# Rotary embedding in an eight-sublayer float32 kernel: half-turned copies by transfers within SBUF in place of matrix products

## What is computed

```python
def rope(x, positions):
    half = x.shape[-1] // 2                       # 32
    inv_freq = ROPE_THETA ** (-jnp.arange(half, dtype=jnp.float32) / half)
    ang = positions.astype(jnp.float32)[:, :, None] * inv_freq
    cos = jnp.cos(ang)[:, :, None, :]
    sin = jnp.sin(ang)[:, :, None, :]
    xf = x.astype(jnp.float32)
    x1, x2 = xf[..., :half], xf[..., half:]
    return jnp.concatenate([x1 * cos - x2 * sin, x2 * cos + x1 * sin], axis=-1).astype(x.dtype)
```

## Time and profile before

| | us |
|---|---|
| median of 3 runs | 3043.06 (3040.68 to 3043.27) |
| the profiled execution | 3038.69 |
| its span, first to last instruction | 3036.9 |
| TensorE busy | 3004.3 (99%) |
| VectorE busy | 1773.7 (58%) |
| ScalarE busy | 1267.4 (42%) |
| GpSimd busy | 146.0 (5%) |
| mean granted TensorE clock, share of full | 0.991 |
| q1, the queue of the weights | 254.52 MB, 26.6% of 16 DMA engines |

### The profile page before, as it was taken

One profiled execution on the slowest core, in us unless ns is written; L12 is line 12 of the kernel. 1 busy time (PEld: TensorE's weight loads), 2 busy tenths in 40 slices (PEclk: granted clock), 3 DMA queues, 4 the chain that ended last, 5 costly groups with the idle time before them and its releaser, 6 DMA issues.

```text
span 3036.9 us, 37846 instructions
## 1 busy us (share of the span) xinstructions
PE 3004.3 (99%) x14656; PEld 2400.7 (79%) x14656; DVE 1773.7 (58%) x3123; ACT 1267.4 (42%) x2374; POOL 146.0 (5%) x203
## 2 busy tenths in 40 slices
PE   9999999999999999999999999999999999999998
PEld 7678888878888888888876677888788766788886
DVE  4565775345555577634465557775364655577743
ACT  4444443322333344332366534543233655354431
POOL 1000000000000000001001101000020011010000
PEclk9999999999999999999999999999999999999999
DMA  4122323322222333333211132322232111223332
GB/s 158 61 98 95 100 98 97 97 77 83 84 77 85 96 98 97 98 97 96 94 36 42 48 98 77 104 97 97 84 99 91 34 44 49 90 84 104 97 97 70
DMA packets 72035, 260.35 MB, mean 86 GB/s; under 512 B 8112, under 2 KB 8112, under 8 KB 71728
## 3 DMA queue, kind: packets, MB, share of 16 engines
q1 hardware_dynamic: 70992, 254.52, 26.6%
q10 hardware_dynamic: 864, 3.41, 0.3%
HBM read 255.81 MB, written 2.10 MB: 85 GB/s over the span
## 4 chain that ended last, share of the span: by engine, by line
PE 93%; DVE 4%; ACT 2%; issue 1%; DMA 0%; POOL 0%; SPq 0%; DVEq 0%
PE bank L469 25%; PE bank L472 24%; PE bank L476 24%; PE bank L546 2%; PE bank L550 2%; PE bank L547 2%; PE bank L626 2%; PE bank L658 2%; PE bank L640 1%; PE bank L782 1%; PE bank L899 1%; DVE wl L1356 1%; DVE big L1931 1%; PE bank L929 1%; PE bank L581 1%
## 5 line engine op out<-in xcount | busy, mean ns | idle before, releaser
L1356 DVE TENSOR_TENSOR wl<-ring,wh 128x512 fp32r<-128x512 f32 (+1 forms) x944 | 647.6, 692 | 822.1 <-ACT wh L985 817.3
L469 PE MATMUL bank<-xh,wh 128*128 128x512 f32 x2464 | 987.7, 401 | 14.2 <-ACT xh L992 7.2
L472 PE MATMUL bank<-xh,wl 128*128 128x512 f32 x2464 | 965.3, 392 | 0.3 <-DVE wl L1356 0.3
L476 PE MATMUL bank<-xl,wh 128*128 128x512 f32 x2464 | 925.7, 391 | 0.0
L985 ACT ACTIVATE wh<-ring 128x512 fp32r<-128x512 f32 (+1 forms) x944 | 579.6, 622 | 807.7 <-PE bank L476 726.4
L469 PEld LDWEIGHTS bank<-xh,wh 128*128 128x128 f32 x2464 | 465.4, 189 | 149.6 <-issue 38.4
L476 PEld LDWEIGHTS bank<-xl,wh 128*128 128x128 f32 x2464 | 465.0, 189 | 100.3 <-DVE xl L1449 0.4
L472 PEld LDWEIGHTS bank<-xh,wl 128*128 128x128 f32 x2464 | 466.0, 189 | 91.1 <-DVE wl L1356 1.3
L469 PE MATMUL bank<-bigr,wh 128*128 128x512 f32 x1024 | 399.0, 390 | 0.6 <-ACT bigr L1339 0.6
L472 PE MATMUL bank<-bigr,wl 128*128 128x512 f32 x1024 | 398.4, 389 | 0.0
L476 PE MATMUL bank<-bigr,wh 128*128 128x512 f32 x1024 | 393.4, 389 | 0.0
(11 more groups left out here) (199 smaller groups left out, 2767.9 us busy)
## 6 DMA issues: line engine op xcount, KB each, us to landing
ring<-in_w_up SPq DMA_DIRECT2D x176, 512.0 KB, 3.5
ring<-in_w_down SPq DMA_DIRECT2D x88, 512.0 KB, 3.5
ring<-in_w_in SPq DMA_DIRECT2D x64, 512.0 KB, 3.5
ring<-in_w_ret SPq DMA_DIRECT2D x32, 512.0 KB, 3.3
ring<-in_w_even SPq DMA_DIRECT2D x19, 512.0 KB, 3.4
ring<-in_w_ret_v SPq DMA_DIRECT2D x16, 512.0 KB, 3.3
ring<-in_w_ret_out SPq DMA_DIRECT2D x16, 512.0 KB, 3.4
ring<-in_w_proj SPq DMA_DIRECT2D x16, 512.0 KB, 3.5
```

The costliest lines, as they stand in the source:

```text
L469: e.matmul(o, K.wh(p, c * 128, 128), oh, start=start, stop=False, skip_group_check=True)
L472: e.matmul(o, K.wl(p, c * 128, 128), oh, start=False, stop=False, skip_group_check=True)
L476: m = e.matmul(o, K.wh(p, c * 128, 128), ol, start=False, stop=stop, skip_group_check=True)
L1356: e.tensor_tensor(K.wl(i, 0, w), K.raw(i), K.wh(i, 0, w).bitcast(F32), ALU.subtract).then_inc(F.lo.tell(("piece", i)), 1)
```

## The change

Each half-turned tile is now written by four transfers of 32 partitions within SBUF, issued by SP, from the scratch tile into a tile of its own in `PP` (`turned(r)`). The minus sign moves from the permutation into `invf`, and so into the sines. TensorE's products and their banks go away. SP gets a wait on VectorE's scaling r ahead of each four transfers; the transfers for r = 0 and 1 stand ahead of unit u+1 in SP's program, those for 2 and 3 ahead of u+2, for 4 ahead of u+3, for 5 and 6 ahead of u+4. Two flags, rot0 for even and rot1 for odd r, tell that the transfers have landed. VectorE's multiplication by the sines reads and writes `turned(r)` in SBUF.

```diff
-for _name, _n in (("ident", 128), ("ones", 128), ("tri", 128), ("neg", 128), ("rot", 128), ("blk", 2), ("mhalf", 64),
+for _name, _n in (("ident", 128), ("ones", 128), ("tri", 128), ("neg", 128), ("blk", 2), ("mhalf", 64),
...
+    def turned(self, r):
+
+        return self.PP[:, r * S:(r + 1) * S]
+
+    def turning(self, r):
+        return (self.F.rot0, self.F.rot1)[r % 2]
...
+    def half_turn(l, r):
+
+        q.wait_ge(F.dve, ("ra", l, r))
+        for a, b in ((0, 32), (32, 0), (64, 96), (96, 64)):
+            e.dma_start(K.turned(r)[a:a + 32, :], K.tmp(2 * r % 4)[b:b + 32, :]).then_inc(
+                K.turning(r).tell(*([("rot", l, r)] if a == 96 else []), by=16), 16)
+
+    turns = {}
+    for l in range(2):
+        u = W.raws["w1", l, 0]
+        turns.update({u + 1: (l, (0, 1)), u + 2: (l, (2, 3)), u + 3: (l, (4,)), u + 4: (l, (5, 6))})
     for u, (src, width, pieces) in enumerate(W.units):
+        if u in turns:
+            for r in turns[u][1]:
+                half_turn(turns[u][0], r)
...
-        def rotated(r):
-
-            b = 2 + (r + 1) % 2
-            q.wait_ge(F.dve, ("ra", l, r))
-            empty(b)
-            e.matmul(BK[b][:, :], K.cs("rot"), K.tmp(2 * r % 4), start=True, stop=True).then_inc(F.attn.tell(("rot", l, r)), 1)
-            vacated[b] = [(F.dve, ("rb", l, r))]
-
...
-        rotated(0)
-        rotated(1)
         tile(("n", l, 6), DT, xn(s), F.dve)
-        rotated(2)
-        rotated(3)
         tile(("n", l, 7), DT, xn(s), F.dve)
-        rotated(4)
...
-            if i == 0:
-                rotated(5)
-                rotated(6)
...
         def rope(r):
-            q.wait_ge(F.attn, ("rot", l, r))
-            e.tensor_tensor(K.tmp(2 * r % 4 + 1), BK[2 + (r + 1) % 2][:, :], K.ROPE[:, S:2 * S], ALU.mult).then_inc(
-                F.dve.tell(("rb", l, r)), 1)
+            q.wait_ge(K.turning(r), ("rot", l, r))
+            e.tensor_tensor(K.turned(r), K.turned(r), K.ROPE[:, S:2 * S], ALU.mult).then_inc(F.dve.tell(("rb", l, r)), 1)
             q.wait_ge(F.dve, ("rb", l, r))
             q.wait_ge(F.pool, ("ra", l, r))
-            e.tensor_tensor(K.ropes[r], K.tmp(2 * r % 4), K.tmp(2 * r % 4 + 1), ALU.add).then_inc(
+            e.tensor_tensor(K.ropes[r], K.tmp(2 * r % 4), K.turned(r), ALU.add).then_inc(
                 F.dve.tell(("rope", l, r)), 1)
...
         def rope(r):
             q.wait_ge(F.dve, ("ra", l, r))
-            q.wait_ge(F.attn, ("rot", l, r))
+            q.wait_ge(K.turning(r), ("rot", l, r))
             e.tensor_tensor(K.tmp(2 * r % 4), K.tmp(2 * r % 4), K.ROPE[:, 0:S], ALU.mult).then_inc(
...
-    put("invf", np.tile(inv, 4)[:, None])
+    put("invf", np.tile(np.concatenate([-inv, inv]), 2)[:, None])
```

More of the change, by code:

```diff
@@ L45 @@
 FLAGS = ("proj", "stat", "attn", "hi", "act", "lo", "dve", "pool", "land0", "land1", "land2", "land3",
-         "x0", "first", "x1", "x2", "x3", "x4", "gain", "cst", "vec", "pos", "dil", "ret", "out")
+         "rot0", "rot1", "x0", "first", "x1", "x2", "x3", "x4", "gain", "cst", "vec", "pos", "dil", "ret", "out")
 class Flag:
@@ L2048, in constants @@
     put("neg", -np.ones((128, 128)))
[L2049 to L2055, removed]
     put("blk", (p[:, None] // 64 == np.arange(2)[None, :]).astype(np.float32))
```

## The result

The changed kernel is slower: 3050.18 us median of 9 runs (3048.98 to 3055.19) against 3039.39 for the kernel before in 9 runs (3035.44 to 3043.27). The ratio is 1.0035, 95% interval 1.0025 to 1.0044, or +10.8 us. Forecast were 3041 us and a range of 3032 to 3048, so both the side and the range were missed. The forecast was counted from a median of 3043.06 in three runs; the kernel before is 3.7 us lower in these nine, so the change itself is the better measure: -2.2 us forecast, +10.8 measured. The profiled executions are 3049.32 and 3038.69 us, 10.6 apart, so the traces hold the whole loss.

A forecast was written before the change was run, and what follows sets the result against it. TensorE, busy 99% of the span, was taken to bound the kernel. After 12.4 us of products removed and the new waits, layer 0 nets -3.0 and layer 1 +0.8: -2.2 from 3043.06 gives 3041 us, range 3032 to 3048.

The forecast's parts named there:

- The products: TensorE's 14 permutation products, removed: 6.21 us in layer 0 and the same in layer 1, at most 12.4 us won.
- The tm unit: First tm load, queued in SP behind the last turns: TensorE waits; layer 0 nets -3.0 us, layer 1 +0.8.
- The scalings: Scalings 0, 2, 4, 6 share a scratch tile and form a chain of period 2.85 + 3.5 = 6.35 us.
- The two multiplications: VectorE's sine and GpSimd's cosine multiplications run one after the other; together they would save 0.65 us per step.
- The traffic: 56 transfers of 64 KB add 3.5 MB beside 254 MB in the same queue: counted as nothing.
- The pitch of the issues: Spacing of SP's four transfer issues per turned tile: taken as 0.38 us, bounds 0.1 and 0.57.
- The landing: Last issue to arrival of a 64 KB transfer within SBUF: taken as 1.6 us, ends 1.4 and 3.4.
- Two ends of the range: Pitch 0.57 with landing 2.1 gives +4 us; multiplications run together give about -7.
- It waits 3.2 us: Layer 0: TensorE, through the compressions at 1425.2, waits 3.2 us until tm can start at 1428.4.
- a wait of 2.2 us for the last units of w1: Layer 1: unit u+3, behind r = 4's transfers, lands at 2255.0; the compression of values wants it at 2252.8.
- Rival (c): Slower: landing of the fourth transfer, sharing the queue with 512 KB loads; at 3.4 us each +8 to +9, 3052; chance 0.10.
- (a): Own forecast: the chain of turned tiles through SP's order gives back most; net -6.1 to +6.1 us; chance 0.64.

The follow-up runs named there:

- version with pairs and late transfers: Changed kernel with own scratch tiles, common transfers for tiles 0/1, 2/3, 4/5 (16 issues a layer, not 28), every turn one unit later; 3032.80 us, 0.9977.
- second filler kernel: Changed kernel plus unread products: 4 before tm and 3 before w1's last unit per layer, 4 before layer 1's compressions; 3046.36 us, 1.0022.

## Why the prediction was wrong, step by step

**What held.** The products are worth 6.2 us a layer (in layer 1 a kernel without transfers gets 4.8, with 1.2 of waits left). The tm unit stands behind the transfers of r = 5 and 6, and TensorE waits for it in both layers. The scalings are a chain through SP, VectorE and GpSimd. The two multiplications exclude each other. The traffic was taken for nothing, which is not quite so: transfers and loads that were issued close together slowed each other (3.1 to 3.9 us for the transfers of r = 5, 4.4 for the load of u+3).

**Where the missing time stands.** In the times of the kernel before, TensorE began tm at 1431.1 in layer 0 (forecast 1428.4, before 1431.4) and at 2266.7 in layer 1 (forecast 2261.7, before 2260.9): 7.7 us later than forecast in the two, so that up to there the sum is +5.5 and not -2.2. The other 6.3 us came behind that point, where the prediction had nothing.

**The pitch of the issues, "I take it for 64 KB too ... I take 0.38"**, is the term that was mis-sized: it measured 0.62 to 0.64, outside its bounds of 0.1 and 0.57. The row taken, 0.33 us, is of loads from HBM on 128 partitions; nothing within SBUF was in the trace. By the prediction's own sensitivity (0.1 us is worth 2.6) this is +6.2 to +6.8. **The landing** was 2.0, not 1.6, worth +2.4. Together they turn -2.2 into about +7, near the +5.5 at which TensorE began tm. In layer 1 the delay is not spread over the periods: scaling 4 ended at 2250.3 in the times of before (forecast 2249.7), and then one landing of 3.4 us and one issue of 1.73 made the rest. The Trainium skill, "DMA: Bandwidth & Descriptors", section on the anatomy of one DMA, gives for the gpsimd path 2.0 us and bytes over 436 GB/s, from which 2.15 us for 64 KB is an estimate; the trace has 2.0, nearer to it than my 1.6. With it the issue would still have been missed.

Two ends of the range were added up wrongly: by the same sensitivities 0.57 and 2.1 give +5.7, not +4, and the two multiplications side by side give -6.1, not about -7.

**The clock was not in the sum.** "It waits 3.2 us" took an idle time at its own length. After the waits TensorE ran at the lower level: the same 256 products of the compressions took 12.74 us in layer 1, and 7.66 at full clock in the version with pairs and late transfers, 5.1 us more; and tm's first products were slowed in both layers. The second is loss; the first only filled time in which TensorE would have waited for tm, as the second filler kernel shows.

**Two waits were overlooked.** In layer 1 the first compression writes a bank that scaling 4 must first have emptied (3.45 us). The prediction's own times had this wait in them: scaling 4 ends at 2249.7, and TensorE would start the compression at 2251.36 - 4.31 = 2247.1. I asked who waits for a scaling only by way of SP. In the changed kernel this wait, too, lies ahead of a tm that comes no earlier without it; with the transfers one unit later, where tm is in time, it is what is left, with slow compressions behind it (3.50 and 12.63 us; the stretch is 3.2 us over before). In its place the prediction had a wait of 2.2 us for the last units of w1, which did not come. In layer 0 the 1.31 us for ScalarE's late copy stand behind the start of tm and are loss.

The account of TensorE's time, from idle rows and the windows:

| us | layer 0 | layer 1 |
|---|---|---|
| products removed | -6.2 | -6.2 |
| TensorE's idle time | +7.05 (1.63 + 4.11 + 1.31) | +6.99 (3.45 + 3.54) |
| compressions at half clock | +0.2 (2.27 - 2.06) | +5.1 (12.74 - 7.66) |
| tm at half clock | some +2.8 | some +2.9 |
| sum | +3.85 | +8.8 |
| measured | +3.3 | +8.5 |

The two entries for tm are estimates: its products start 0.23 us apart at half clock and 0.13 at full. The 2.06 are the last 64 products of the compressions at full clock, in the second filler kernel. The table says what TensorE did with its time, not what each entry would save alone: in layer 1 the bank's wait and the slow compressions stand in for a longer wait for tm. Of the cost of the transfers in the two stretches, 22.7 us over the kernel without them, some 12.8 are idle time (14.0 less the 1.2 of that kernel) and some 11 the clock that follows it (1.1 us too many, the size of the error of such a sum).

Rival (c) came true in its side and near its size (3052 forecast), which is luck, for its mechanism did not: landing was 2.0 us in the median, and over 3 for 8 of the 56, most of them close to a load. The mechanism was (a)'s, with a larger pitch and the clock on top. The chance of 0.10 for slower was too low because that rival left the pitch out: its upper end, 0.57, was read from loads with waits between them and taken for a ceiling, and with 2.1 of landing it made only +4 (+5.7 when added up rightly).

## What to carry to other kernels

A transfer that waits for an engine and stands in the queue of the weight loads costs its issue time and its wait to every load behind it; price the number of issues, not the bytes, and put them behind the loads that someone needs soon. Moving work off an engine that sets the time can cost more than it saves when it opens idle time on it: list who waits for each late result, its banks as well as its data, add the clock behind each gap, and then ask which of the waits ends last, since only that one is loss. Fewer and wider transfers, placed late, with scratch tiles of their own and tm's low parts ahead of rope 5, gave 10.5 us from the same idea that lost 10.8 with many narrow ones placed early.

## What the runs showed of the hardware

- SP needs 0.51 to 0.59 us to issue a 64 KB transfer of 32 partitions within SBUF (up to 1.73 in this kernel), more than the 0.33 for a 512 KB load and the 0.465 for 256 KB within SBUF on 128 partitions. A load right behind such transfers takes 0.46.
- A transfer of 64 KB within SBUF lands in 2.0 us; in layer 0 the four right behind a 512 KB load took 3.1 to 3.9, and the load 4.4 instead of 3.7. In the version with pairs and late transfers, four of 128 KB took 2.3 to 2.4 where no load was near (1408.73) and 4.7 to 4.9 right behind one (1412.10).
- The clock fell to half about 5 us after an idle time of 3.45 us had begun (2250.1), when TensorE had been busy again for more than a microsecond, and stayed there for some 20 us. The 256 products that took 12.74 us there and 7.66 at full clock began at full clock too: the first 49 started 0.029 us apart, those behind the fall 0.053, a factor of 1.8 and not 2 for these products of 32 columns. The Trainium skill, "TensorE: Matmul & The Clock Gate", Part 1, has a clock gate that sets TensorE's rate, full or half, by how busy it has been; the trace agrees with that.
- Unneeded products in the idle time, 18 over both layers, kept the clock at 1.00 through both stages (1425 to 1440 and 2249 to 2270); 12 of them made the kernel 3.6 us faster.
- VectorE's multiplication with two SBUF inputs and GpSimd's ran one after the other: GpSimd's took 1.74 us instead of 1.27 when VectorE's had begun 0.11 earlier (1408.68 and 1408.79).
